# Input products of the second block of rows moved into a kernel's opening

## The reference

```
h   = rmsnorm(x) ;  xl, gl, us = h @ w_in            # 1024 -> 3 x 512
xc  = conv4(xl) ;   r, i = sigmoid(xc @ wa), sigmoid(xc @ wx)
hl  = scan(exp(-8 r softplus(-lam)), sqrt(1 - a^2) * i * xc)
y1  = hl * gelu(gl)
g   = gelu(S5(us))                                   # complex diagonal states, 32 groups
y2  = g * sigmoid(g @ w_glu)
x   = x + [rmsnorm(y1), rmsnorm(y2)] @ w_out
x   = x + (silu(h2 @ w_gate) * (h2 @ w_up)) @ w_down # h2 = rmsnorm(x), 1024 -> 2816
y   = rmsnorm(x)
```

## Time and profile before

| | us |
|---|---|
| median of 3 runs | 2331.46 (2329.62 to 2332.35) |
| time of the profiled execution | 2331.18 |
| span of its profile | 2329.4 |
| PE busy | 2205.3 (95%) |
| PE weight loads busy | 2119.3 (91%) |
| DVE busy | 1542.1 (66%) |
| ACT busy | 1090.7 (47%) |
| POOL busy | 410.2 (18%) |
| last `s5` product of the opening ends | 196.0 |
| first FFN product of block 0 begins | 276.1 |

### The profile page before, as it was taken

The page is one execution under the profiler, slowest core; times in us unless marked ns, Lnnn a source line. Parts: engine busy times, 40 slices in busy tenths (PEclk is TensorE's granted clock), DMA queues, the critical chain, the costliest instruction groups (busy, mean ns, idle before and its releaser), DMA issues.

```text
span 2329.4 us, 30360 instructions
## 1 busy us (share of the span) xinstructions
PE 2205.3 (95%) x11650; PEld 2119.3 (91%) x11650; DVE 1542.1 (66%) x2581; ACT 1090.7 (47%) x1458; POOL 410.2 (18%) x459
## 2 busy tenths in 40 slices
PE   4876799999999999999999999999999999999996
PEld 2555799999999999999999999999999999999996
DVE  8667546578756656875766578766658875665544
ACT  3444434654634455564444664644455563432232
POOL 6433101024011101321010023111102321100001
PEclk9977899999999999999999999999999999999998
DMA  5762333546333545553353655334455643343331
GB/s 171 210 169 77 115 117 115 152 154 191 123 111 117 176 125 162 168 166 109 117 172 106 151 175 174 127 113 141 152 138 156 173 135 109 117 147 109 124 121 58
DMA packets 200527, 322.81 MB, mean 139 GB/s; under 512 B 89088, under 2 KB 131712, under 8 KB 200256
## 3 DMA queue, kind: packets, MB, share of 16 engines
q1 hardware_dynamic: 200256, 320.65, 45.5%
q0 software_dynamic: 128, 0.23, 0.0%
HBM read 296.39 MB, written 26.53 MB: 139 GB/s over the span
## 4 chain that ended last, share of the span: by engine, by line
PE 88%; DVE 5%; POOL 2%; ACT 2%; issue 1%; DMA 1%; SPq 1%; POOLq 0%; DVEq 0%; ACTq 0%
PE acc L814 27%; PE acc L816 27%; PE acc L815 26%; PE acc L879 3%; PE acc L901 1%; POOL tmp L545 1%; PE acc L900 1%; PE acc L910 1%; DVE rstd L1093 1%; PE acc L890 1%; PE acc L872 1%; DVE w_hl L976 1%; DVE s5prod L976 0%; DMA u<-z_dram 0%; DVE act_hl L976 0%
## 5 line engine op out<-in xcount | busy, mean ns | idle before, releaser
L814 PE MATMUL acc<-act_hl,w_hl 128*128 128x416 f32 x2544 | 905.1, 356 | 18.1 <-DVE act_hl L976 18.1
L816 PE MATMUL acc<-act_hl,w_hl 128*128 128x416 f32 x2544 | 895.2, 352 | 0.0
L815 PE MATMUL acc<-act_hl,w_hl 128*128 128x416 f32 x2544 | 892.4, 351 | 0.0
L976 DVE TENSOR_TENSOR w_hl<-w_raw,w_hl 128x1024 fp32r<-128x1024 f32 x428 | 532.0, 1257 | 78.9 <-ACT w_hl L634 77.6
L814 PEld LDWEIGHTS acc<-act_hl,w_hl 128*128 128x128 f32 x2544 | 479.9, 189 | 29.1 <-issue 16.3
L815 PEld LDWEIGHTS acc<-act_hl,w_hl 128*128 128x128 f32 x2544 | 480.0, 189 | 9.7 <-issue 5.0
L634 ACT ACTIVATE w_hl<-w_raw 128x1024 fp32r<-128x1024 f32 x428 | 443.6, 1051 | 78.6 <-DMA w_raw<-in_w_in 43.4
L816 PEld LDWEIGHTS acc<-act_hl,w_hl 128*128 128x128 f32 x2544 | 479.7, 189 | 0.6
L976 DVE TENSOR_TENSOR x_acc<-x_acc,acc 128x416 f32<-128x416 f32 x480 | 272.9, 585 | 199.1 <-PE acc L816 192.3
L545 POOL TENSOR_TENSOR tmp<-tmp 128x416 f32<-128x416 f32 x135 | 168.3, 1246 | 1123.3 <-ACT tmp L642 1113.3
L814 PE MATMUL acc<-ff_hl,w_hl 128*128 128x416 f32 x880 | 312.3, 355 | 14.8 <-DVE x_acc L976 12.0
(11 more groups left out here) (155 smaller groups left out, 1894.2 us busy)
## 6 DMA issues: line engine op xcount, KB each, us to landing
w_raw<-in_w_ffn SPq DMA_DIRECT2D x330, 512.0 KB, 3.7
w_raw<-in_w_in SPq DMA_DIRECT2D x60, 512.0 KB, 3.4
w_raw<-in_w_out SPq DMA_DIRECT2D x40, 512.0 KB, 3.3
s5y<-y_dram SPq DMA_DIRECT2D x80, 256.0 KB, 4.1
s5t<-t_dram SPq DMA_DIRECT2D x64, 162.0 KB, 3.9
s5v<-v_dram SPq DMA_DIRECT2D x80, 128.0 KB, 3.8
x_acc<-in_x SPq DMA_DIRECT2D x4, 1664.0 KB, 7.3
out_y<-x_acc SPq DMA_DIRECT2D x8, 832.0 KB, 6.5
```

The costliest lines, as they stand in the source:

```text
L814: pe.matmul(out, w(0), x(0), start=first, stop=False)
L815: pe.matmul(out, w(0), x(1), start=False, stop=False)
L816: return pe.matmul(out, w(1), x(0), start=False, stop=last)
L976: return v.tensor_tensor(out, x, y, op)
```

## The change

- The 12 input units of block 1 are made in the opening, as plain float32 products of the raw weights with `rows1` (the test `b == 0` becomes `b < 2`). For that block 1's rows are loaded once more, early, into `rows1` (step `xr`), squared (`sq1` of block 1), normed in place (`h1` of block 1). `rows0` and `rows1` lie where the split rows of block 0 (`act_hl0`) come later.
- Their results are kept: `us` in `zs_next`, `xl` and `gl` in `kept`, over block 1's `act_hl1`. The mixer of block 1 has its own list `SECOND`, without `sq1`, `n1`, `h1`, `us`, `xl`, `gl` and `zst`; its new step `xc` copies `xl` from `kept` (ACT). `zst` of block 1 is the second last step of the opening. The load of block 1's rows into `x_acc1` moves from the end of the opening to just before `s5` 0.
- Phases are made for two groups of pairs at once, one per partition half: `tb`, `ts`, `tr`, `tt` run for 0 and 1 only. `ts` has one more sine, `tt` has 12 stores of 64 partitions in place of 3 of 128.
- The sum over chunks of `n1` for blocks 0 and 1 is made by eight matmuls with ones instead of seven POOL adds and one matmul. In every norm the root comes first, by ACT straight from PSUM with mean and epsilon in its scale and bias; then DVE's reciprocal. DVE's mean instruction (L1091) is gone.
- `FIRST` has a new order, and `MIXER` (for blocks 2 to 4) moves some steps by one to four places. In the opening `glu` 1 now comes right after `glu` 0, and `ns` after `oa` 0. Block size, the FFN, its weights and the ring stay.
- `T0` (416, like `T`), `width()`, `cols5()`, `here()` only name sizes; with these values they change nothing. Some buffers change place.

The core of the diff:

```diff
+def sums(which, b):
+    return 0 if which == "n1" and b < 2 else NCH[which] - 1
...
-                rows = at("rows", [P, KD, T], F32, top[0])
+                rows0 = at("rows0", [P, KD, T], F32, top[0])
+                rows1 = at("rows1", [P, KD, T], F32, top[0] + 4 * KD * T)
+            else:
+                kept = at("kept", [P, KD, T], F32, top[0] + 4 * KD * T)
...
+        tau = sb("tau", [P, 3, GP])
+        rho = sb("rho", [P, GP])
...
+        tq = [[at(f"tq{i}", [P, GE, W5], F32, YL + 4 * i * GE * W5) for i in range(3)] + [sb("tq3", [P, GE, W5])]]
+        tq.append([at(f"tq{4 + i}", [P, GE, W5], F32, U5 + 4 * i * GE * W5) for i in range(3)] + [sb("tq7", [P, GE, W5])])
...
                 if kind == "x" and b:
                     if b >= 2:
                         sp.wait_ge(y_st[b % 2], 32 * (b // 2))
+                    else:
+                        sp.wait_ge(pl_done, 1)
                     load_x(b)
+                elif kind == "xr":
+                    sp.dma_start(rows1[:, :, 0:T], a["x"][0][:, :, here(1)]).then_inc(next_in, 16)
...
-                    for n, (done, src) in enumerate(((cos_done, 1), (sin_done, 2), (trho_done, 0))):
+                    for n, (done, first, second) in enumerate(((cos_done, 1, 1), (sin_done, 2, 3), (trho_done, 0, 0))):
                         sp.wait_ge(done, j + 1)
-                        sp.dma_start(t_dram[:, j * GE // 2:(j + 1) * GE // 2, n],
-                                     tq[j % 2][src][:].rearrange("p (t q) c -> p t q c", q=2)).then_inc(t_st[n][j % 2], 16)
+                        for half in range(2):
+                            t = half * GP // 2 + j * GE // 2
+                            for rows_, src in ((slice(0, NP_), first), (slice(NP_, P), second)):
+                                sp.dma_start(t_dram[rows_, t:t + GE // 2, n],
+                                             tq[j][src][half * NP_:(half + 1) * NP_].rearrange("p (t q) c -> p t q c", q=2))\
...
+                    sp.dma_start(z_dram(b).rearrange("e g h s c -> (g h) e (s c)"),
+                                 (zs_next if b == 1 else zs(b))[:].rearrange("p e s c -> p e (s c)")).then_inc(z_st, 16)
...
+                if not sums(which, b):
+                    act.activation(first_sq(b, k), src, ACT.Square).then_inc(sq_done, 1)
+                    return
...
-            def root(which, b):
-                act.wait_ge(rec_done, NORM_N[(which, b)] + 1)
-                act.activation(rstd[:], rstd[:], ACT.Sqrt).then_inc(rstd_done, 1)
+                act.activation(tmp[:, 6 + k % 2, 0:width(b)], src, ACT.Square).then_inc(sq_done, 1)
+            def root(step):
+                bank, tk = wait_m(act, step), width(step[1])
+                if step == ("n1", 1, 0):
+                    act.wait_ge(h_made, KD)
+                act.activation(rstd[:, 0:tk], acc[:, bank, 0:tk], ACT.Sqrt, bias=sm(EPSC), scale=1.0 / (NCH[step[0]] * P))\
+                   .then_inc(m_freed(step), 1)
...
-                    act.activation(q2[:], q0[:], ACT.Sin, scale=sm(NS2PI)).then_inc(sin_done, 1)
+                    act.activation(q2[:], q0[:], ACT.Sin, scale=TWO_PI)
+                    act.activation(q3[:], q0[:], ACT.Sin, scale=-TWO_PI).then_inc(sin_done, 1)
...
+                    elif (kind, b, j) == ("sq1", 1, 0):
+                        wait_m(act, ("n1", 0, 0))
+                        act.wait_ge(next_in, 16)
...
-                    act.activation(natural(zs[:, j]), tokens(acc[:, bank, 0:T]), ACT.Copy).then_inc(m_freed(step), 1)
+                    act.activation(natural((zs_next if b == 1 else zs(b))[:, j]), tokens(acc[:, bank, 0:tk]), ACT.Copy).then_inc(m_freed(step), 1)
+                elif kind == "xc":
+                    act.wait_ge(conv_done, b * KL + j)
+                    act.activation(xl[:, 3:3 + tk], kept[:, KL + j, 0:tk], ACT.Copy).then_inc(xc_done, 1)
...
-                    if b < LAST:
-                        act.activation(xl[:, 3:3 + T], acc[:, bank, 0:T], ACT.Copy).then_inc(m_freed(step), 1)
+                    if b == 1:
+                        act.wait_ge(x_in[1], 16)
+                        act.activation(kept[:, KL + j, 0:tk], acc[:, bank, 0:tk], ACT.Copy).then_inc(m_freed(step), 1)
+                    elif b < LAST:
+                        act.activation(xl[:, 3:3 + tk], acc[:, bank, 0:tk], ACT.Copy).then_inc(m_freed(step), 1)
...
                         act.wait_ge(nrm_lo, 2 * KL * b)
+                    elif b == 1:
+                        act.wait_ge(x_in[1], 16)
+                    elif j == 0:
+                        for n in range(3):
+                            act.wait_ge(t_st[n][0], 64)
                     bank = wait_m(act, step)
-                    act.activation(y_lru[:, j, :], acc[:, bank, 0:T], ACT.Gelu_apprx_tanh).then_inc(m_freed(step), 1)
+                    act.activation((kept if b == 1 else y_lru)[:, j, 0:tk], acc[:, bank, 0:tk], ACT.Gelu_apprx_tanh).then_inc(m_freed(step), 1)
                 elif kind == "ga":
...
-                        wait_m(act, ("gl", b, KL - 1))
-                    act.activation(tokens(act_hl[b % 2][:, 0, KL + j, :]), natural(zs[:, j]), ACT.Copy).then_inc(g_hi, 1)
+                        for k in ("us", "xl", "gl"):
+                            wait_m(act, (k, b, KL - 1))
+                            if b == 0:
+                                wait_m(act, (k, 1, KL - 1))
+                    act.activation(tokens(act_hl[b % 2][:, 0, KL + j, 0:tk]), natural(zs(b)[:, j]), ACT.Copy).then_inc(g_hi, 1)
                 elif kind == "ml":
...
+                    if not sums(kind, b):
+                        bank = m_bank(step)
+                        for k in range(KD):
+                            pe.wait_ge(sq_done, SQ_AT[(kind, b)] + k + 1)
+                            ins = pe.matmul(acc[:, bank, 0:tk], ones[:], first_sq(b, k), start=k == 0, stop=k == KD - 1)
+                        ins.then_inc(m_full, 1)
+                        continue
...
+                    if b < 2:
                         for k in range(KD):
                             if j == 0:
-                                pe.wait_ge(h_made, k + 1)
...
+            def reciprocal_root(step):
                 wait_evacuated(v, step)
-                v.reciprocal(rstd[:], rstd[:]).then_inc(rec_done, 1)
+                tk = width(step[1])
+                v.reciprocal(rstd[:, 0:tk], rstd[:, 0:tk]).then_inc(rstd_done, 1)
...
+                if b == 1:
+                    v.wait_ge(nrm_lo, 2 * KL)
+                tt(y_lru[:, j, 0:tk], (kept if b == 1 else y_lru)[:, j, 0:tk], h, MUL).then_inc(ylru_done, 1)
...
+                    if (kind, b) not in HL_AT:
                         for k in H_PARTS[j]:
-                            stt(rows[:, k, :], x_acc[0][:, k, :], v1(gain + k), rstd[:], MUL, MUL)\
+                            stt(rows(b)[:, k, 0:tk], (rows1 if b else x_acc[0])[:, k, 0:tk], v1(gain + k), rstd[:, 0:tk], MUL, MUL)\
...
-                    wait_evacuated(v, ("xl", b, j))
+                    if b == 1:
+                        v.wait_ge(xc_done, j + 1)
+                    else:
```

More of the change, by code:

```diff
@@ L19 @@
 TB = TP + TS
[L21 removed]
+NB, T0, T = 5, 416, 416
 LAST = NB - 1
[L23 removed]
+TPL = SEQ - T0 - (LAST - 1) * T
 L = 8
@@ L65, in steps @@
 def steps():
-    out = [(kind, 0, j) for kind, j in FIRST] + [("x", 1, 0)]
+    out = [(kind, b[0] if b else 0, j) for kind, j, *b in FIRST]
     for b in range(NB):
@@ L80, in steps @@
             if b + 1 < NB:
-                out += [(kind, b + 1, j) for at, (kind, j) in MIXER if at == place]
+                out += [(kind, b + 1, j) for at, (kind, j) in (MIXER if b else SECOND) if at == place]
     out += [("dn", NB * NPAIR - 1, h) for h in range(2)]
@@ L98, with raw, split_here @@
 NU = len(SRC)
-NRAW = 3 * KL
-assert all(k in ("us", "xl", "gl") and not b for k, b, _ in SRC[:NRAW])
-NOWN, EARLY = 6, 4
-assert SRC[NRAW:NRAW + NOWN] == [("glu", 0, 0), ("glu", 0, 1)] + [("out", 0, j) for j in range(EARLY)]
+EARLY = 4
+def raw(kind, b, j):
+    return kind in ("us", "xl", "gl") and b < 2
+SPLIT = {u: i for i, u in enumerate(u for u, s in enumerate(SRC) if not raw(*s))}
+OWN = list(SPLIT)[:2 + EARLY]
+assert [SRC[u] for u in OWN] == [("glu", 0, 0), ("glu", 0, 1)] + [("out", 0, j) for j in range(EARLY)]
+def split_here(u):
+    return u < NU and u in SPLIT and u not in OWN
 def early(kind, b, j):
```

314 lines of the change are left out of this document (167 added, 147 removed).

## The result

The changed kernel takes 2316.22 us (median of 4 runs, 2315.78 to 2316.70) against 2330.86 for the kernel before, run beside it: a ratio of 0.9937, with a 95% interval of 0.992 to 0.9954. It is faster by 14.6 us. Forecast was 26.0. The range of 2293 to 2321 holds the result; the narrower 2298 to 2311, which the forecast had by itself, does not. Some 11 us of the expected gain are missing, and the question of this study is where they went.

What follows compares the result with a forecast made beforehand. PE's own work bounds the kernel from block 0's FFN on; the opening has holes. Opening +26.2, full part -54.6, new waits +3.0, last norm -0.6: -26.0 us, so 2305.5 us, range 2293 to 2321.

Steps and rivals of the forecast that it cites:

- The two prices: Each moved unit takes 4.5 us from the full part and puts 5.8 us into the opening; 53.9 out, 69.6 in.
- The latency lies under the units: Opening's S5 part: units between dependent steps cover most of 36.4 us latency and low clock; 112.3 us in place of 72.6.
- The 2.5 us for the clock and the 4 for banks and late operands: Opening's S5 part: additions to 105.8 us of work, for low clock after the `u5` wait and for remaining latency.
- the rival of the other sign: S5 part keeps its latency and units add to it: 142.2 us, kernel 2335; slower once past 138 us. Chance 6%.
- the opening gives nothing: Rival: DVE late, `s5` 0 stays at 123.4, tail loses only three means; 11.7 us less gained, 2317. Chance 15%.
- The tail: Last S5 step to first FFN product: 8.1 us shorter, from 3.8 wait, 2.5 matmuls and 1.8 for three means.
- The term for the order: Opening's tail: `glu` 1 no longer behind `oa` 0 saves a 3.8 us wait and 2.5 us of matmuls.
- the sentence that `nl` comes no earlier: Opening's tail: `nl` itself comes no earlier, since POOL still adds its squares.
- the 3 us of new PE waits: Block 1's S5 steps in the full part: 3 us of new PE waits, between 0 and 8, from late DVE.
- what gets tighter is DVE: Block 1's S5 steps: 95.2 us of DVE in 97.5 us of PE, full to 98%.
- The first rival: Block 1's S5 steps: DVE's instructions or gaps a tenth longer when closer, 9.5 us more, 2315. Chance 18%.
- The moved steps of `MIXER` I count at nothing: Blocks 2 to 4: moved steps cost 0, as these blocks keep all PE work and have hardly a wait to lose.

Runs made afterwards that it cites:

- experiment 3: The changed kernel with all 12 moved units ahead of the first S5 step instead of between the S5 steps: 2356.14 us, ratio 1.0112.
- experiment 9: The changed kernel with the old order at the opening's end (`glu` 1 behind `oa` 0, `ns` behind `oa` 2): 2323.22 us, ratio 0.9978.
- experiment 4: The kernel before with only the new norms (root first in every norm, DVE's mean gone): 2337.35 us, ratio 1.0029.
- experiment 2: The changed kernel with block 1's mixer steps of places 26 to 52 spread over places 8 to 52, same order: 2328.9 us, ratio 0.9994.
- experiment 7: The changed kernel with three moves in `SECOND` (`xc` 0 and `cv` 0 earlier, `xc` 3 behind `s5` 3, last S5 steps later): 2308.41 us, ratio 0.9919.
- experiment 6: The changed kernel with old norms in blocks 2 to 4 and block 1 except `n1`, last `nf` kept new, and old `MIXER`: 2314.57 us, ratio 0.9927.
- experiment 1: The changed kernel with the old `MIXER` list for blocks 2 to 4: 2320.58 us, ratio 0.9962.

## Why the prediction was right in kind and wrong in size

- **The two prices** (5.8 us in, 4.5 us out) hold. Two units in a row took 11.41 us in the S5 part, and the moved units ahead of `s5` 0 took 68.0 for twelve in experiment 3, where the prediction had 69.6. The price out has no row of its own; waits and clock explain 11.3 of the 12.5 us that were missing from the 54.6, so it is right within some 1.2 us in all.
- **The latency lies under the units.** This was the main argument and it held better than forecast: 105.1 us where the sum of the work alone was 105.8. The 2.5 us for the clock and the 4 for banks and late operands were hardly needed: PE was idle for 1.5 us, and a unit at 68.0 / 12 = 5.67 us instead of 5.8 saved 1.9 over the 14. Experiment 3 shows the other side: take the units from between the steps and 33 of the 36.4 us are back. With that the rival of the other sign is refuted by its own condition (138 us and more; it was 105.1). So is "the opening gives nothing": the S5 part began 4.1 us earlier, of 5.4 forecast. Where the 1.3 us are I did not follow.
- **The tail** was forecast at 8.1 and gave 5.3. The term for the order was right, 6.3 (experiment 9). What was wrong is the sentence that `nl` comes no earlier and, unsaid, no later: its matmul started 7.8 us after PE had gone idle, before 5.6. The other branch had become late: DVE's last product of `ld` 3 comes at 225.0, behind the last S5 product, and two POOL additions of 4.05 us from 228.1 (3.27 before) follow before `nl` can start at 232.2. That is 2.2 us of the 2.8 missing. The rest fits the mean of `nl`, which the prediction counted with 0.6: in experiment 4, where only the norms differ, this stretch took 79.1 us instead of 79.9, not 1.8 less.
- **The step that failed is the 3 us of new PE waits, between 0 and 8**, in "what gets tighter is DVE". Block 1's stretch was short by 9.5 us: 12.5 in place of 3. Of these, 6.5 are new waits, twice the forecast but inside its bounds, 4.8 are the clock, which the prediction did not price at all, and 1.2 stay open. The two waits of 2.2 and 1.2 us at 467.4 and 537.4 are what the clock fell behind. The reasoning took an average, DVE full to 98%, and looked for waits for the low parts of weights. DVE was busy for 81% of block 1's S5 steps, as before, and those waits came to nothing there. What counted was who stands in front of whom, and a sign of it stood in the trace before: the 12.0 us for `x_acc`, which the prediction passed over when it called 7.1 us the largest wait. When the twelve units went, the places of the mixer lost the long PE work between them, and single steps came to stand directly in front of an addition to `x_acc` or of a gelu that frees a bank. That the units' going did this is argued, from the order of the lists; what the experiments show is that the order decides: experiment 2 spread the same steps and the time got worse, experiment 7 moved eight steps and got 8.2 us back.
- **The first rival** gave 2315, nearly the measured time, but for a reason that fell, so the agreement is luck. Its mechanism was that DVE's instructions or their gaps get longer when they stand closer. They did not: in block 1's stretch the low parts take 1221 ns after and 1238 before, and POOL's `s5p` in the opening takes 746 after and 877 before. DVE's idle time before its S5 products, where nothing that the profile shows held it up, is 2.6 us in the 80 from 440 to 520, and 6.5 in the 80 of the earlier trace rows. The Trainium skill (SBUF — State Buffer, Who interferes with whom) says that a DVE instruction with two SBUF inputs and a POOL instruction that reads SBUF contend. The trace agrees for single instructions: DVE's low part at 222.1 us takes 1.22 us, the one at 229.4, beside POOL's additions, 1.79. But the packing of block 1's stretch did not make it more frequent, as the mean shows. The groups of DVE from 440 to 520 us and of POOL from 119 to 225 us, by count, busy time and mean, and the rows of that contention:

```profile
L1088 DVE TENSOR_TENSOR w_hl<-w_raw,w_hl 128x1024 fp32r<-128x1024 f32 x13 | 15.9, 1221 | 0.5 <-ACT w_hl L716 0.4
```

```profile
L655 POOL TENSOR_TENSOR s5p<-s5w,s5t 128x216 f32<-128x216 f32 x16 | 11.9, 746 | 97.4 <-DVE s5w L1266 97.4
```

```profile
222.09 1.22 DVE L1088 TENSOR_TENSOR w_hl<-w_raw,w_hl 128x1024 fp32r<-128x1024 f32 x1
...
229.44 1.79 DVE L1088 TENSOR_TENSOR w_hl<-w_raw,w_hl 128x1024 fp32r<-128x1024 f32 x1 [0.23 <-ACT w_hl L716]
```

```profile
228.10 4.05 POOL L629 TENSOR_TENSOR tmp<-tmp 128x416 f32<-128x416 f32 x2 [0.74 <-ACT tmp L727]
```

- **"The moved steps of `MIXER` I count at nothing"** was wrong the other way round, and covered a second failure. Blocks 2 to 4 lost 6.4 us, and most of it is the norms', which the prediction had counted as a gain of 0.6 each on the path and at nothing elsewhere. Experiment 4 shows them costing 1.4 to 5.1 us per woven mixer, experiment 6 gives 4.2 back, and against experiment 1, with the same `MIXER`, 5.9. In the changed kernel itself the 6.4 us are 3.2 us of new waits and 1.7 of clock, granted 0.66 from 1846 to 1851 us behind a wait of 1.8; 1.5 are not placed. A help of the moved steps of `MIXER` against it is possible and not shown. Leaving out DVE's mean saves 0.6 us on the path of the opening; the root that now stands first brought a table load in front of a copy that PE needs less than 5 us later.
- **Luck** is in the size. The range holds the result because the losses, 9.5 and 6.4 us, were partly paid by an opening that ended 3.3 us better than forecast and by 1.5 us at the end that are the clock's.
- **What stays open**: why PE waits in block 4's S5 steps in experiment 6, behind which most of the remaining 2.2 us are lost, and the 1.6 to 2.3 us that block 1 loses with the old norms. Its list `SECOND` may be laid out for the new ones; that was not tried. Of the some 4 us by which experiment 1 is slower, the profile places only 1.7 in blocks 2 to 4.
